# A two-block network on one core: stage openings run three units together, scan set-up and some TensorE work moved

## The reference

```python
# first block, per layer
h = rms_norm(x, norm1_g[l]) * (1.0 + sc1) + sh1
q, k, v, iq, ik, iw, z, xbc, dt_raw, ga, gm = split(h @ w_in[l])
o_attn = dsa_attention(rope(norm(q)), rope(norm(k)), v, iq, ik, iw, 64) @ w_attn_o[l]
xs, bm, cm = split(silu(causal_dwconv(xbc, ...)))
y = ssd_scan(xs * dt, A * dt, bm, cm)          # 32 heads, decay = exp(segsum(cumsum(a)))
y = rms_norm((y + xs * d_skip) * silu(z), ssm_norm_g)   # in 4 groups of 512 channels
x = x + g1 * ((sigmoid(ga) * o_attn + sigmoid(gm) * (y @ w_ssm_o[l])) @ w_out[l])
h = rms_norm(x, norm2_g[l]) * (1.0 + sc2) + sh2
val, gate = split(causal_dwconv(h @ w_up[l], ...))
x = x + g2 * ((silu(gate) * val) @ w_down[l])
# second block, per layer
h = rms_norm(x, norm1_g_2[l])
o = three mixers of h @ w_in_2[l]: latent attention, gated linear attention,
    and S5: a diagonal complex recurrence over 256 steps, 32 groups of 64 states
x = x + gated_sum(o) @ w_out_2[l]
x = x + square(relu(rms_norm(x, norm2_g_2[l]) @ w_ff1_2[l])) @ w_ff2_2[l]
```

## Time and profile before

| | |
|---|---|
| median of 3 runs | 2456.28 us (2456.2 to 2458.23) |
| the profiled execution, its own time | 2457.06 us |
| its span in the trace | 2455.0 us |
| granted TensorE clock, mean | 0.964 |
| busy: PE, DVE, ACT, POOL | 94%, 72%, 55%, 11% |
| matmul instructions in the trace | 17392 |

### The profile page before, as it was taken

The page is one execution under the profiler, slowest core; times in us unless marked ns, Lnnn a source line. Parts: engine busy times, 40 slices in busy tenths (PEclk is TensorE's granted clock), DMA queues, the critical chain, the costliest instruction groups (busy, mean ns, idle before and its releaser), DMA issues.

```text
span 2455.0 us, 42466 instructions
## 1 busy us (share of the span) xinstructions
PE 2300.1 (94%) x17392; PEld 2144.8 (87%) x17392; DVE 1772.0 (72%) x3151; ACT 1362.2 (55%) x2140; POOL 266.8 (11%) x308
## 2 busy tenths in 40 slices
PE   2999999999999999999999898898999888898999
PEld 2988899999988898999999786798999775798999
DVE  5797668578659877675674889885654988886653
ACT  3577886466446888754664436444543436444542
POOL 0000000022000000000110243300000333300000
PEclk9999999999989999999999899999999899899999
DMA  7544456556645454564655413243555313243553
GB/s 278 172 165 163 155 187 213 185 188 229 227 166 168 152 187 149 186 220 144 188 174 182 135 59 107 95 149 118 189 189 172 121 61 107 94 155 122 188 186 124
DMA packets 110849, 395.73 MB, mean 161 GB/s; under 512 B 12320, under 2 KB 13888, under 8 KB 110400
## 3 DMA queue, kind: packets, MB, share of 16 engines
q1 hardware_dynamic: 96768, 343.52, 42.3%
q0 software_dynamic: 12160, 44.08, 5.5%
q10 hardware_dynamic: 1728, 5.43, 0.6%
HBM read 391.93 MB, written 1.05 MB: 160 GB/s over the span
## 4 chain that ended last, share of the span: by engine, by line
PE 76%; DVE 16%; ACT 3%; POOL 2%; issue 2%; DMA 1%; SPq 0%; DVEq 0%; ACTq 0%
PE bank L524 76%; DVE WL L1360 3%; ACT scr L933 1%; DMA ring<-in_w 1%; DVE arena L1424 1%; ACT L924 1%; POOL arena L2033 1%; PE bank L595 1%; POOL arena L2037 0%; POOL arena L2035 0%; DVE scr L1407 0%; DVE arena L1528 0%; DVE scr L1527 0%; ACT WH L933 0%; DVE arena L1958 0%
## 5 line engine op out<-in xcount | busy, mean ns | idle before, releaser
L933 ACT ACTIVATE WH<-ring 128x1024 fp32r<-128x1024 f32 (+1 forms) x638 | 670.1, 1051 | 894.5 <-PE bank L524 869.5
L524 PE MATMUL bank<-HTH,WH 128*128 128x256 f32 x3392 | 1000.7, 295 | 42.6 <-DVE HTL L1400 14.9
L524 PE MATMUL bank<-HTL,WH 128*128 128x256 f32 x3392 | 977.0, 288 | 0.0
L524 PE MATMUL bank<-HTH,WL 128*128 128x256 f32 x3392 | 976.3, 288 | 0.0
L1360 DVE TENSOR_TENSOR WL<-ring,WH 128x1024 fp32r<-128x1024 f32 (+2 forms) x616 | 745.1, 1217 | 202.2 <-ACT WH L933 200.6
L524 PEld LDWEIGHTS bank<-HTH,WH 128*128 128x128 f32 x3392 | 667.6, 197 | 75.6 <-issue 54.7
L524 PEld LDWEIGHTS bank<-HTL,WH 128*128 128x128 f32 x3392 | 669.5, 197 | 2.0 <-issue 1.4
L524 PEld LDWEIGHTS bank<-HTH,WL 128*128 128x128 f32 x3392 | 668.3, 197 | 0.0
L924 ACT ACT_TABLE_LOAD x114 | 146.3, 1283 | 47.3 <-PE bank L524 22.5
L524 PE MATMUL bank<-scr,cst 128*128 128x256 f32 (+2 forms) x304 | 96.4, 446 | 53.6 <-ACT scr L933 53.4
L524 PE MATMUL bank<-ff2h,WH 128*128 128x256 f32 x512 | 145.4, 284 | 0.0
(11 more groups left out here) (274 smaller groups left out, 3865.2 us busy)
## 6 DMA issues: line engine op xcount, KB each, us to landing
ring<-in_w SPq DMA_DIRECT2D x620, 512.0 KB, 3.7
arena<-in_wada POOLq DMA_DIRECT2D x80, 512.0 KB, 4.8
ring<-in_w SPq DMA_DIRECT2D x16, 384.0 KB, 3.7
arena<-in_wada SPq DMA_DIRECT2D x8, 512.0 KB, 19.4
arena<-in_wada ACTq DMA_DIRECT2D x8, 512.0 KB, 21.8
ring<-in_w SPq DMA_DIRECT2D x8, 288.0 KB, 2.8
arena<-in_s POOLq DMA_DIRECT2D x4, 512.0 KB, 4.1
cst<-in_cst SPq DMA_DIRECT2D x1, 1025.0 KB, 6.2
```

The costliest lines, as they stand in the source:

```text
L524: ins = e.matmul(out, a, b, start=(start and i == 0), stop=(stop and i == len(pairs) - 1))
L933: return e.activation(out, a, func, **kw)
```

## The change

Six edits. (1) The first three units of every stage run together (`opening`): TensorE waits for the low halves of all three, and then for each chunk does the nine matmuls of the three units. DVE makes the third unit's low half one slot earlier. (2) ACT's `boundary` begins with a load of the table set of Ln and Exp. (3) The squares of chunks 0 to 5 are added on DVE into one tile, and one matmul sums it; after the last stage they are not made. (4) In `gate` DVE adds two pairs of squares, and two matmuls stay of four. (5) The row of decay is split in two rounded halves, stored below each other in `csr` (64 rows, 64 more are zero), and picked with one rounded matmul by a selector `picks` of 128 rows. (6) The parameter pieces of `s5` become `s5set` and move into the stage before (slots 48 to 62 of stage 3, 38 to 52 of stage 5), POOL's loads of the parameters and its first two table steps move with them, and the 32 pieces of the scan start at slot 6 and stand 1.6 units apart.

```diff
-    "s5": [1, 2, 3, 4, 5, 6, 7, 8] + turn_ticks(11, 32, 3, 2) + [59, 60, 61, 62, 63],
+    "s5": turn_ticks(6, 32, 8, 5) + [57, 58, 59, 60, 61],
 }
+S5_TICKS = {stage_b: [48, 50, 52, 54, 56, 58, 60, 62], stage_d: [38, 40, 42, 44, 46, 48, 50, 52]}
...
 ssd on TensorE
-                mm(b[0:32, 256:512], [(adt[:, 0:32], tri)], stop=False)
+                mm(b[0:64, 256:512], [(adt2[:, 0:64], tri)], stop=False)
...
-                            pick = con("id", rows_=32)[:, 2 * c + hh:2 * c + hh + 1].to_broadcast([32, 128])
-                            ins = mm(L.b[0][:, hh * T:hh * T + T], [(pick, csT)])
+                            pick = picks[:, 2 * c + hh:2 * c + hh + 1].to_broadcast([128, 128])
+                            ins = mm(L.b[0][:, hh * T:hh * T + T], [(pick, csr[:, :])])
...
 gate on TensorE
-                for j in range(4):
-                    ins = mm(L.b[1][:, 0:T], [(con("ones"), L.s[j // 2][:, T * (j % 2):T * (j % 2) + T])],
-                             start=(j == 0), stop=(j == 3))
+                mm(L.b[1][:, 0:T], [(con("ones"), L.s[0][:, T * j:T * j + T]) for j in range(2)]).then_inc(
...
+            def opening(xs):
+                for x in xs:
+                    p.wait_ge(lo_done(x))
+                    if x.first and x.group.before:
+                        p.wait_ge(bank_free(x.group.before))
+                for k in range(8):
+                    p.wait_ge(chunk_ready(xs[0], k))
+                    for x in xs:
+                        ...
+                        mm(o, [(wh[:, k, :], HTH[:, k, :]), (wh[:, k, :], HTL[:, k, :])], start=(k == 0 and x.first),
+                           stop=False)
+                        ins = mm(o, [(wl[:, k, :], HTH[:, k, :])], start=False,
+                                 stop=(k == 7 and (x.last or alone)))
...
-                if g and g.kind == "res" and g.gi < 3:
-                    for c in (2 * g.gi, 2 * g.gi + 1):
-                        p.wait_ge(norm_scalar("sq", g.stage + 1, c))
-                        sums(c, square_tile(c), g.stage + 1)
+                if g and g.kind == "res" and g.gi == 2 and g.stage < 7:
+                    p.wait_ge(norm_vector("sq", g.stage + 1, 2))
+                    sums(5, square_sum, g.stage + 1, start=True)
...
 boundary on ACT
+                act(None, None, None)
...
 evac on DVE
+                elif s == 1 and k == "res" and st < 7:
+                    p.wait_ge(norm_scalar("sq", st + 1, 2 * gi + 1))
+                    t = scr[:, 5 + gi % 2, :]
+                    if gi == 0:
+                        ins = e.tensor_tensor(square_sum, t[:, 0:T], t[:, T:512], ALU.add)
+                    else:
+                        p.wait_ge(norm_vector("sq", st + 1, gi - 1))
+                        serial(e.tensor_tensor(square_sum, square_sum, t[:, 0:T], ALU.add), norm_vector)
+                        ins = e.tensor_tensor(square_sum, square_sum, t[:, T:512], ALU.add)
...
 gate on DVE
+                p.wait_ge(L.A("gsq", l, g))
+                e.tensor_tensor(L.s[0], L.s[0], L.s[1], ALU.add).then_inc(L.V.inc("gsq", l, g), 1)
...
 the loop of DVE
-                if u + 2 < len(units) and units[u + 2].split and not units[u + 2].pool:
-                    lo(units[u + 2])
+                for v in (() if u in plan.base else (u + 2, u + 3) if u + 1 in plan.base else (u + 2,)):
+                    if v < len(units) and units[v].split and not units[v].pool:
+                        lo(units[v])
...
 the loop of POOL
+                    if u == plan.base[4 + 2 * l] - 1:
+                        turns(l, (0, 1))
...
-                        turns(l)
+                        turns(l, range(2, 8))
```

More of the change, by code:

```diff
@@ L488, in program @@
                             agenda.setdefault(plan.base[st] + s, []).append((name, l))
+        for l in range(2):
+            st = 3 + 2 * l
+            for s in S5_TICKS[STAGES[st][0]]:
+                agenda.setdefault(plan.base[st] + s, []).append(("s5set", l))
         ada_at = {}
@@ L496, in act_set @@
         def act_set(x):
-            return 6 if x in (ACT.Ln, ACT.Exp) else 18 if x in (ACT.Silu, ACT.Tanh, ACT.Sin) else None
+            return 6 if x in (ACT.Ln, ACT.Exp, None) else 18 if x in (ACT.Silu, ACT.Tanh, ACT.Sin) else None
         def sync_program(e):
@@ L525, in mm, with sums @@
                 return ins
-            def sums(c, tile, st, n=8):
-                ins = mm(bank[4][:, 0:T], [(con("ones"), tile)], start=(c == 0), stop=(c == n - 1))
+            def sums(c, tile, st, start):
+                ins = mm(bank[4][:, 0:T], [(con("ones"), tile)], start=start, stop=(c == 7))
                 ins.then_inc(sums_done.inc("sum", st, c), 1)
@@ L535, in boundary @@
                         p.wait_ge(in_cst("in"))
-                    sums(c, square_tile(c), st)
+                    sums(c, square_tile(c), st, start=(c == 0))
             def attn(l, L, par):
@@ L758, in s5 @@
                 L = LC
-                for i in range(8):
-                    yield
                 def inputs(q, h):
@@ L894, in tensor_program @@
                     next(live[key])
-                unit(units[u])
+                if u in plan.base:
+                    opening(units[u:u + 3])
+                elif u - 1 not in plan.base and u - 2 not in plan.base:
+                    unit(units[u])
             assert all(next(s, "end") == "end" for s in live.values())
@@ L1144, in ssd @@
                 yield
+                p.wait_ge(L.P("cs", l))
+                act(csr[0:64, :], L.b[0][0:64, 256:512], ACT.Copy).then_inc(L.A.inc("cshi", l), 1)
                 yield
@@ L1325, in scalar_program @@
             act(trig[:, 0, :], y, ACT.Sin).then_inc(start_scalar.inc("trig"), 1)
+            p.wait_ge(in_cst("in"))
+            for r in (slice(0, 32), slice(32, 64)):
+                act(picks[r, :], con("id")[r, r], ACT.Copy).then_inc(start_scalar.inc(*(("pick",) if r.start else ())), 1)
             live = {}
@@ L1989, in vector_program @@
                 if u == 0:
-                    lo(units[0])
-                    lo(units[1])
+                    for x in units[0:3]:
+                        lo(x)
                 if u in plan.base:
@@ L2021, in turns @@
                 p.wait_ge(LC.V("tf", l))
-                for q in range(8):
+                for q in qs:
                     if q > 1:
```

88 lines of the change are left out of this document (60 added, 28 removed), and 4 rows, old and new, of the table IK.

## The result

| | before | changed |
|---|---|---|
| median | 2457.26 us (4 runs) | 2393.39 us (4 runs, 2392.69 to 2398.07) |
| the profiled execution's span | 2455.0 us | 2390.6 us |
| ratio | | 0.9743, 95% interval 0.9726 to 0.9759 |
| granted clock, mean | 0.964 | 0.971 |
| busy: PE, DVE, ACT, POOL | 94%, 72%, 55%, 11% | 93%, 75%, 56%, 12% |

A forecast was written before the change was run, and what follows sets the result against it. The prediction took TensorE as the bound (76% of the chain that ended last), with DVE setting the pace in some stretches. Its terms summed to 63.7 us off 2457.06, giving 2393 us; likeliest case 2383 to 2405, wider range 2368 to 2427.

The forecast's parts named there:

- picks: Decay rows in stages 0 and 2: 0.9 us saved in each of 24 steps, taken as 18 us, ends 0 and 29.
- squares: Sums of squares around the stage boundaries: 37 fewer on TensorE at 0.43 us each, 16 us, ends 12 and 18.
- gates: Gates: 16 sums fewer on TensorE, 6.9 us by price, taken as 3.5 us for DVE's added work, ends -3 and 7.
- table load: Boundaries of stages 2, 4, 5 and 7: load hidden in ACT's wait for the residual, 4 by 1.28, 5.1 us.
- openings: First three units of each stage run together: gain less waits of the fifth unit, 1 us, ends -8 and +12.
- stages 4 and 6: Scan parameters moved out, scan earlier and wider: 14 us a stage (9 plus 5), 28 for both, ends -10 and +60.
- stage 3: Moved pieces delay DVE, so TensorE waits 4.7 us at the last early sum; 5.5 us lost with the clock, ends 0 and 14.
- POOL in stage 4's boundary: POOL's table operations slow DVE's additions ahead of and in the first chunks: 3 us lost, ends 0 and 8.
- B: ACT and DVE become the bound in stages 0 and 2, stages 4 and 6 stay slow: 35 us gained, 2421; chance 0.20.
- C: Cheaper picks open gaps and the clock falls in the dense stretches: slower than before, 2515 with half affected; chance 0.03.
- D: Moved parameters only move the cost: stage 3 stalls by 14, stage 4's boundary by 8; 2406; chance 0.10.
- A: Waits of stages 4 and 6 go whole: 30 us a stage, openings 6, 2356; chance 0.19.

The follow-up runs named there:

- e1: Changed kernel with the decay rows picked by two 32-row float32 matmuls again, without split halves or the tile `picks`; 2418.7 us, 24.6 us slower than the changed kernel.
- e2: Changed kernel with the six early sums of squares back on TensorE and no adds on DVE; 2399.8 us, 5.7 us slower than the changed kernel.
- e5: Changed kernel with the gates' four squares summed by four matmuls and the norm's table loaded in front of Ln again; 2405.5 us, 11.3 us slower.
- e4: Changed kernel with a stage's first three units run one behind the other again; 2393.2 us, ratio 0.9739 to the kernel before, no difference told from the changed kernel.
- e3: Changed kernel with the scan's parameters back in stages 4 and 6, scan from slot 11 at spacing 1.5, POOL's tables and DMAs there; 2405.2 us, 11.1 us slower.
- e8: Changed kernel with the scan's parameters in twelve smaller pieces from slot 6 of stage 3 and 8 of stage 5, POOL's first tables at slots 56 and 44; 2389.7 us.
- e6: Changed kernel with the parameters still in stages 3 and 5, but the scan back at slot 11 and spacing 1.5; 2379.4 us, 14.7 us faster than the changed kernel.
- e9: Changed kernel with the scan from slot 11 at 1.5, last early sum behind the stage's last unit, parameters in thirteen pieces; median 2369.34 us, 24.8 us faster.

## Why the prediction was right, point by point

The time came out to the microsecond, and the mechanism is the forecast's: TensorE's own list made shorter in its dense stretches, and a set-up taken off a full DVE and paid for in part in stage 3. That it came out so closely is luck. Stages 4 and 6 gave 7.4 us less than was forecast, and a term that the forecast did not have gave 7.1: the matmuls that read the arena became faster. The two cancelled.

| term | forecast | measured | from |
|---|---|---|---|
| picks | 18 | 17.4 (24.6 less the 7.2 of the arena's matmuls); 18.1 by slots 24 to 70 | e1 |
| matmuls that read the arena | nothing | 7.1 | before, changed, e1 |
| squares | 16 | 12.0 (stages 0, 1, 2, 4, 5, 6), some 2 in stage 3 by the price, 2.6 for the six behind the last stage | e2; the last from slots 34 to 64 of stage 7, 88.96 us before and 86.40 in e1 |
| gates | 3.5 | 3.0 | e5 |
| table load | 5.1 | 5.5 | e5 |
| openings | 1 | 0, within 5 | e4 |
| stages 4 and 6 | 28 | 20.6 (10.4 + 8.9 and the 1.3 of POOL's line) | e3 |
| stage 3 | -5.5 | -8.2 | e3 |
| POOL in stage 4's boundary | -3 | -1.3 | e3, e8 |

*Picks.* Right in size, with two steps of the working off. A step saves 0.82 us and not 0.9, since two picks cost 0.34 and not 0.24, and the deduction for ACT was nearly unneeded. What was left out is what `picks`, a tile of 128 bytes a partition, did to the matmuls that read the arena.

*Squares and gates.* The price of 0.43 holds wherever it can be read. DVE's adds cost nothing that can be seen, except in stage 3 and for some 0.2 us in each of the gaps in front of stages 1, 3, 5 and 7 (5.41, 5.41, 5.22 and 5.22 us, against 5.20, 5.20, 5.01 and 5.01 in e2).

*Table load.* Right in size, and by the trace's 1.28 and not by a drain on top of it. The Trainium skill's drain of 1.38 us a switch (ScalarE: Activation LUTs, What ACT_TABLE_LOAD costs) appears in none of the four gaps of e5: they are longer by 1.28, and it would have made them 2.66. The places were off: stage 6 needs it since the parameters moved, and in stage 4 most of it lies under another wait.

*Stage 3.* Right in place and kind: the wait for DVE at the last early sum was put at 4.7 us, and 5.09 were found. Its size was off, because the sum of 5.5 allowed 0.8 for the clock. The clock fell for 6.8 us, and the units behind it also waited for their low halves.

*The scan parameters in stages 4 and 6: the step that failed.* "In the stretches after it the scan's wider spacing takes one or two pieces out of each 24 slots; I take 5." Against e3, which has the parameters in place and the scan from slot 11, the slots from 16 on of stages 4 and 6 are 1.6 and 4.5 us longer in the changed kernel, and not 5 shorter. Slots 32 to 79 are 8.0 and 4.8 shorter, but slots 16 to 32 are 9.6 and 9.2 longer. The other half of the term, 9 for the first stretch with its three additional pieces, was too low: slots 0 to 16 are 12.0 and 13.4 shorter, in stage 4 with the 1.3 of POOL's line already taken off. The sum, 14 a stage, came within 5 of the 10.4 and 8.9 that were measured. e6 shows what the earlier and wider scan did to the gain: with the scan left alone, the parameters' leaving gives 14.7 and 1.3 for the boundary in stage 4, and 17.2 in stage 6.

*Openings.* The gain of the first three units and the waits of the fifth are both there, and undoing them moves nothing that can be measured. No run shows a gain of some 5 us, against which the forecast's 1 us sets the two waits: the first 72 matmuls of the stages take 8.2 us less than in the kernel before (81.1 against 89.2) and 8.9 less than in e4, and each of the two waits is 1.5 and not 2. In the kernel before, 13 to 27 of the first 48 matmuls of a stage stood in a stretch at 1.2 GHz.

Of the rivals, B (the neighbours take over) is refuted by e1 for the picks, C by the clock in 182 to 335 us, D by e3 and e6. A (stages 4 and 6 give 30 each) is not what happened, but e6 and e9 go part of its way: with the scan at 11 stages 4 and 6 are 332.6 long in e9, 21 and 22 under the kernel before.

What stays open: why the openings' 8.9 us are given back, of which only the 3.0 of the two waits and the 0.8 of the gaps have a name; what in the spacing of 1.6 holds slots 24 to 32 of stages 4 and 6; and whether the place of the arena alone makes its matmuls faster, which a tile of 128 bytes that nothing uses would show.

## What to carry to other kernels

Moving work off a full engine and starting what depends on it earlier are two edits; try them apart, for the second can take back a third or a half of what the first gives. When a sum or any other step of the busiest engine is made to wait for a second engine, look at what else was put into that engine's queue in the same change: neither the adds nor the moved pieces stalled stage 3 alone. When undoing an edit costs more than its working says, look at the code that it did not touch: here every stage had a part of the surplus, and it came with a small tile. And where identical code gets different amounts of the low clock, read a small term from its own slots, not from the total.

## What the runs showed of the hardware

The low clock is spread unevenly over identical work. Slots 0 to 8 of stage 2 are the same code in the changed kernel and in e8, and begin at nearly the same time (678.18 and 678.42 us), yet take 35.8 and 39.2 us. The first has 6.8 us at 1.2 GHz, the second 13.7. Their forty microseconds, the changed kernel first:

```profile
678.00:718.00 40.00, 35.93 (x262) 33.79 (x262) 25.69 (x47) 17.87 (x28) 1.05 (x2) 0.91 0.47 156
```

```profile
678.00:718.00 40.00, 35.93 (x235) 34.25 (x235) 24.25 (x42) 15.41 (x25) 1.05 (x2) 0.83 0.44 144
```

TensorE is busy for the same 35.93 us and gets 27 matmuls fewer done. At 0.12 us a matmul against 0.22, 3.4 us at the low clock lose 1.5 us of work, so a comparison of single edits carries some 2 to 3 us a stage that belong to no edit. e3 differs from the changed kernel by 2.3, 1.5 and 1.8 us in stages 0 to 2, where their code is the same and e3 has 3.4 us more of the low clock in each.

Matmuls of one shape and type did not all cost the same. At the full clock the distance between starts was 118.3 ns where the input lay in the arena, in every kernel with the tile `picks`, and 120.0 in the two without it, the kernel before and e1.
